# Reading a float32 accumulator back before the other one is complete: the tail of a routed-expert layer on one core

## The reference, cut to what matters

```python
hid = silu(x @ exp_w_gate[e]) * (x @ exp_w_up[e])          # 64 experts, 8 per token
routed = sum over e of (hid * gate[e]) @ exp_w_down[e]
shared = (silu(x @ shared_w_gate) * (x @ shared_w_up)) @ shared_w_down
x = x + g_f * (routed + shared)                            # g_f: one row per sequence
y = rmsnorm(x, final_norm_g)
```

## Time and profile before

| | us |
|---|---|
| three runs | 855.84, 860.97, 861.21 |
| median | 860.97 |
| profiled execution | 862.52 |
| its span in the trace | 860.6 |
| last weight load landed, about | 805.5 |
| last expert's down product (L1089) | 825.5 to 827.5 |
| first of the six reads issued | 834.62 |
| first final operation of VectorE (L1618) | 839.64 |
| last store issued (L387) | 857.32 |

### The profile page before, as it was taken

The page is one execution under the profiler, slowest core; times in us unless marked ns, Lnnn a source line. Parts: engine busy times, 40 slices in busy tenths (PEclk is TensorE's granted clock), DMA queues, the critical chain, the costliest instruction groups (busy, mean ns, idle before and its releaser), DMA issues.

```text
span 860.6 us, 14556 instructions
## 1 busy us (share of the span) xinstructions
PE 709.4 (82%) x4895; PEld 394.5 (46%) x4896; DVE 324.8 (38%) x617; ACT 227.9 (26%) x385; POOL 310.2 (36%) x331
## 2 busy tenths in 40 slices
PE   2599978999878979999789989988789868896830
PEld 1277553545535545554445545544355334443510
DVE  3105570646812463234142332333422423233217
ACT  4202621123022332233132222222322323232212
POOL 4001021021431663456352553545336443354130
PEclk9789989999879998999999999999999999999985
DMA  9979999308517999999999999999999999999333
GB/s 271 374 265 321 345 374 315 115 28 344 219 39 255 390 399 412 400 380 385 399 393 384 394 394 384 388 405 398 392 386 402 384 386 390 364 385 373 133 85 128
DMA packets 74658, 279.17 MB, mean 324 GB/s; under 512 B 19263, under 2 KB 22459, under 8 KB 48880
## 3 DMA queue, kind: packets, MB, share of 16 engines
q1 hardware_dynamic: 50082, 252.00, 74.5%
q0 software_dynamic: 23264, 26.07, 12.7%
q10 hardware_dynamic: 1262, 0.43, 0.2%
HBM read 272.28 MB, written 26.04 MB: 347 GB/s over the span
## 4 chain that ended last, share of the span: by engine, by line
PE 48%; DMA 43%; DVE 3%; issue 3%; SPq 1%; ACT 1%; POOL 0%; POOLq 0%; DVEq 0%
DMA gu<-in_exp_w_up 35%; PE bank L1053 18%; PE bank L1089 7%; PE bank L817 5%; PE bank L808 4%; DMA gu<-in_ada_w 4%; PE bank L935 3%; DMA gu<-in_w_in 2%; PE bank L1038 1%; PE bank L1135 1%; PE bank L820 1%; PE bank L783 1%; DMA sh<-acc_rows 1%; SPq L327 1%; PE bank L941 1%
## 5 line engine op out<-in xcount | busy, mean ns | idle before, releaser
L1053 PE MATMUL bank<-gu,et 128*64 128x256 f32 x2496 | 290.8, 389 | 59.6 <-DMA gu<-in_exp_w_up 53.8
L1053 PEld LDWEIGHTS bank<-gu,et 128*64 128x64 f32 x2496 | 183.4, 140 | 189.0 <-issue 113.5
L499 POOL DMA_INDIRECT acc_rows<-et,idx x64 | 104.6, 1634 | 283.5 <-DVE et L1544 197.6
L1089 PE MATMUL bank<-dn,et 128*64 128x512 f32 x624 | 150.3, 608 | 15.9 <-issue 13.7
L1537 DVE COPY et<-bank 128x256 f32<-128x256 f32 x64 | 27.2, 424 | 292.3 <-PE bank L1070 292.3
L706 ACT ACTIVATE et<-bank 64x512 f32<-64x512 f32 x64 | 37.9, 592 | 289.5 <-PE bank L1053 289.5
L1089 PEld LDWEIGHTS bank<-dn,et 128*64 128x64 f32 x624 | 41.6, 137 | 81.5 <-issue 80.9
L714 ACT ACTIVATE et<-bank,mb 128x512 f32<-128x512 f32 x64 | 44.0, 687 | 121.3 <-PE bank L1089 113.6
L1544 DVE TENSOR_SCALAR et<-bank,mb 128x512 f32<-128x512 f32 x64 | 48.1, 751 | 67.8 <-PE bank L1089 62.5
L1530 DVE TENSOR_TENSOR et<-et 64x512 f32<-64x512 f32 x64 | 67.9, 1061 | 0.4 <-ACT et L707 0.4
L509 POOL DMA_DIRECT2D small<-halfc x50 | 57.3, 1147 | 0.0
(11 more groups left out here) (279 smaller groups left out, 628.7 us busy)
## 6 DMA issues: line engine op xcount, KB each, us to landing
gu<-in_exp_w_gate SPq DMA_DIRECT2D x64, 1024.0 KB, 14.9
gu<-in_exp_w_up SPq DMA_DIRECT2D x64, 1024.0 KB, 29.6
dn<-in_exp_w_down SPq DMA_DIRECT2D x64, 1024.0 KB, 29.8
gu<-in_ada_w SPq DMA_DIRECT2D x12, 2048.0 KB, 17.4
gu<-in_w_in SPq DMA_DIRECT2D x3, 2048.0 KB, 19.3
gu<-in_w_out SPq DMA_DIRECT2D x2, 2048.0 KB, 28.9
acc_rows<-gn SPq DMA_DIRECT2D x2, 1280.0 KB, 17.1
gu<-in_w_in SPq DMA_DIRECT2D x2, 1024.0 KB, 19.6
```

What stands on the lines that cost most here:

```text
L499: pool.indirect_dma_start(acc_rows[u % 2], bass.IndirectOffsetOnAxis(ap=idx[:, u, 0:1], axis=0), yo[:, u % 2, 0, :], None, bounds_check=2 ...
L1053: mm = pe.matmul(bank[u % 2][64 * c:64 * c + 64, b * FE:(b + 1) * FE], xt[:, b, k % 4, k // 4, :], w[:, (c * KT + k) * FE:(c * KT + k + 1) ...
L1089: mm = pe.matmul(bank[5 + b][64 * c:64 * c + 64, :], hT[:, b, j, :], dn[:, dslot(u), j * D + c * HALF:j * D + (c + 1) * HALF], start=(j == ...
```

## The change

SP waits for the even accumulator's own semaphore, reads the even accumulator, all three tiles, into `sh`; then it waits for `routed` and reads the odd one into `xn`. The sum of the two doesn't depend on which is where. The wait within the branch for a second round of tokens (more than 128 for an expert) is only reached in such a round.

```diff
                     load_dn(r, NE // U - 1, U - 1)
+                    sync.wait_ge(scattered[0], 16 * NE * (r + 1))
                     if r + 1 < ROUNDS:
                         more_rounds(r + 1)
             more_rounds(1)
 
+            sync.wait_ge(s["pre_done"], 3)
+            sync.wait_ge(scattered[0], 16 * NE)
+            for t, (t0, n) in enumerate(TILES):
+                sync.dma_start(sh[0:n, t, :], acc_rows[0][2 * t0:2 * (t0 + n), :].rearrange("(p h) n -> p (h n)", h=2)).then_inc(acc_back[t], 16)
             sync.wait_ge(s["routed"], 1)
-            sync.wait_ge(s["pre_done"], 3)
             for t, (t0, n) in enumerate(TILES):
-                for b, dst in ((0, xn), (1, sh)):
-                    sync.dma_start(dst[0:n, t, :], acc_rows[b][2 * t0:2 * (t0 + n), :].rearrange("(p h) n -> p (h n)", h=2)).then_inc(acc_back[t], 16)
+                sync.dma_start(xn[0:n, t, :], acc_rows[1][2 * t0:2 * (t0 + n), :].rearrange("(p h) n -> p (h n)", h=2)).then_inc(acc_back[t], 16)
```

## The result

The changed kernel takes 860.76 us, the median of 20 runs (856.79 to 862.85), and the kernel before 857.0 us beside it (20 runs, 854.77 to 861.21). The ratio is 1.0039, 95% interval 1.0024 to 1.0054, so 2.1 to 4.6 us slower. The prediction said 0.9 us faster. The time itself is close to the 860.1 predicted, but that is luck: the first three runs of the kernel before (median 860.97), from whose median the 0.9 us were subtracted, lay above the median of its twenty.

The account below looks back on a forecast made before the run. Only the tail could change, bound by tile 1's start. Tile 0 0.15 us later and the idle 1.08 us gone put tile 1 0.9 us earlier: 860.1 us from the median of three runs, range 855.0 to 863.3.

Parts of the forecast that it names:

- What bounds the tail: End of kernel: tile 1's start, the later of VectorE free from tile 0 and tile 1's reads, plus 16.1 us.
- wait in front of tile 1: VectorE's idle time between tiles 0 and 1, awaiting a read into `sh`; forecast to go, worth 1.08 us.
- The start of the even reads: SP's first even read, released by expert 62's second scatter: issued about 832.1 in place of 834.62, 2.5 us earlier.
- Tile 0: First final operations on VectorE, needing the first and fourth reads: start 839.8, ends 838.2 and 841.2, before 839.64.
- half rate: Third tile's 64-partition even read, ahead of tile 0's odd read: 0.26 MB at 200 instead of 350 GB/s, 0.6 us more.
- Rival A: Early start arrives in full at 426 GB/s: tile 0 at 838.2, 2.5 us gained, 858.5; chance 0.15.
- Rival B: Three even reads ahead move tile 0 to about 840.7, paying back the 1.08 us: 861.0; chance 0.25 with D.
- lags: Reads landing behind their nominal ends at 350 GB/s: 1.2, 1.0, 1.5 and 3.0 us for the four full reads.
- Rival C: Even reads delay expert 63's small copy, hence `routed`; tile 0 starts 3.4 us later, +2.3 us, 863.3; chance 0.15.

Follow-up runs that it names:

- l_pool2: Kernel before with even reads of tiles 0 and 1 early, tile 0's even half worked off first, third tile's three final operations on GpSimd: ratio 1.0035.
- e_wait: Kernel before with a wait for the even semaphore added ahead of the wait for `routed`, no read moved: ratio 0.9981.
- b_dead: Kernel before with one more wait, in the never entered branch for a second round; no executed instruction changes: ratio 1.0002.
- m_after: The changed kernel once more, beside other runs of the kernel before: ratio 1.0025.
- d_order: Kernel before with only the new order, all six reads after `routed`, three even then three odd, nothing early: ratio 1.0029.
- i_actqueue: Changed kernel without the wait in the branch, odd reads on ScalarE's queue instead of SP's: ratio 1.0023 to the kernel before.
- c_nodead: Changed kernel without the wait in the never entered branch for a second round: ratio 1.0027 to the kernel before.
- h_t01early: Kernel before with even reads of tiles 0 and 1 early, then odd 0, odd 1, even 2, odd 2 after `routed`: ratio 1.0.
- j_order2: Kernel before with all six reads after `routed`, ordered even 0, even 1, odd 0, odd 1, even 2, odd 2: ratio 1.001.
- n_last: Kernel before with all six reads after `routed`, tile 0's odd read last of all: ratio 1.0088.

## Why the prediction was wrong, point by point

**What bounds the tail** held: tile 1 starts when VectorE has done tile 0 or its own reads are in, and from there on the length is fixed. After, 841.48 to the end of the span is 16.1 us, as before. The wait in front of tile 1 went, as forecast, in every kernel that read the even half first, but for `l_pool2` (1.06 us). What it is worth was taken from one execution, though: the old order shows 1.11 us in the kernel before, 1.53 in `e_wait` and none in `b_dead`.

**The start of the even reads** was forecast 2.5 us ahead of the first read of before. In one execution it was (offset 2.48 in `m_after`), in the profiled one it was 1.26 us (3.81 against 5.07), since expert 62's scatter took 5.6 us to land and not 4.4. That is most of this execution's error in tile 0 (1.3 of 1.5 us): one row doesn't give the range of a wait.

**Tile 0 was the step that failed:** "I take 839.8, nearest to the case with the half rate, with 838.2 and 841.2 as ends." That is offset 10.25, at most 11.65. Measured: 11.74, 12.87 and 14.32. Take it as a start and a length. From the first issue to tile 0 I had 7.7 us (832.1 to 839.8). `d_order`, where nothing is early, took 7.98 (830.88 to 838.86), so for a stream that begins when the scatters are over the sum was right, with the third tile's read in the way (1.35 us by my terms, 0.75 for its bytes and 0.6 for its half rate; 1.6 measured). What failed is the credit for the head start: I let this length begin 2.5 us earlier and kept it. Set against the 2.96 us that the order costs, tile 0 came 1.65, 2.18 (`i_actqueue`), 2.78 and 4.23 us later than before, so the head start gave back 1.3, 0.8 and 0.2 us, and in `m_after` it cost 1.3. These are differences of single executions, so the sizes are rough. In the profiled execution the length was 7.93 us, but the start came 1.3 us later than forecast. Where the start did come early, the length grew: 9.82 us with a start at offset 3.05 (`c_nodead`, 831.04 to 840.86) and 11.84 with 2.48 (`m_after`, 827.56 to 839.40). Between a head start that doesn't come and one that is lost on the way, nothing was left to pay for the third and fourth place of the odd read.

Against a gain of at most 1.08 us from the wait in front of tile 1, a tile 0 that comes 1.65 to 4.2 us later gives a loss of 0.6 to 3.2 us. Set against the means of the old order (tile 1 at 14.66, after at 16.64), it is 2.0 us.

**Rival A** is out: its rate was reached (426 GB/s), its tile 0 at offset 8.65 in no kernel. **Rival B** named the right thing, the three even reads ahead, and stopped at a price of zero; its own lags of up to 3.0 us, which it cited, would have carried it past 840.7. I had put the upper end of tile 0 at 841.2, already on the slow side, and took the middle.

**Rival C** forecast the right sign and nearly the right size (+2.3 us), but by another mechanism, and that one is refuted at its price. It wanted the small copy to land 2.5 us late. In the five kernels whose trace shows `routed` beside early reads it came at offset 4.17 to 5.50, with the copy landing in at most 4.5 us (`h_t01early`); in the six without early reads at 4.40 to 5.07. In the changed kernel and `c_nodead`, where SP was still issuing, it came no later than 6.1 and 4.8. What the Trainium skill says in "DMA: Bandwidth & Descriptors", section "Queues, rings and completion order", of engines taking turns between queues isn't seen at work in `i_actqueue`: by turns I expected tile 0 at 9.5 to 11 there, and it came at 12.27. That the copy's completion write waits for even reads in flight no run here shows.

**The half rate.** By the Trainium skill, page "SBUF — State Buffer", section "Door 1: The DMA port swizzle", 64 partitions reach half of the ports. The 213 GB/s at the end of `j_order2` agree with it; the 147 to 188 in `n_last` are lower still, and full reads moved in that stretch too. For this read the rule and its price were about right (0.6 us, 0.8 measured in one pair of traces); what I didn't draw from them was that this one read, set ahead of the odd one, costs more (1.6 us) than the wait in front of tile 1 that goes (1.08 us).

**What stays open.** The tail accounts for about 2.0 us of a loss measured at 2.1 to 4.6 us in the first comparison and 0.3 to 4.1 in the later two. Whether a part of the first lies elsewhere can't be told from these. Nor is it shown why the first odd read took 5.6 us in one execution and 10.1 in another of the same kernel. A slow first read explains a part of it at most: in `c_nodead` the first one took 3.5 us, and the second 7.0 where `d_order` has 4.5. That reads issued before offset 3 meet busy engines is seen; that this is the reason for the longer streams is only argued. And why none of the kernels with tails of 28.5 to 29.8 us is faster than the kernel before stays open.

## What to carry to other kernels

A transfer that must wait for the last result gets no earlier because others went ahead of it; here it got later. Where a consumer needs one transfer of each group, order them so that each of its inputs is complete as soon as can be, whether or not a group can start early. Narrow transfers (64 partitions) belong behind the wide ones that somebody waits for, since a read of theirs delayed what was behind it by twice what its bytes are worth (1.6 against 0.75 us, in one pair of traces). And with tails that vary by 1.6 to 2.6 us from execution to execution, one profile can show a mechanism but not its size: the first one after the change showed 0.47 us of a loss of 3.3.

## What the runs showed of the hardware that I had not expected

Float32 operations of GpSimd and VectorE on SBUF at the same time slowed each other: from 1.23 to 3.36 us for 128x1024 on VectorE, from 2.33 to 3.2 for 64x1024 on GpSimd, one waiting for the other to end (`l_pool2`). The issue of a DMA on SP's queue can take 2.37 us with reads in flight, against 0.35 on an idle queue. The first read took 4.3 to 6.6 us when it went out within 3 us of the last scatter's issue, and 3.3 to 3.7 later. And in the new order it took 7.98 us from the first issue to tile 0 with nothing early, and 7.93, 9.82, 9.37 and 11.84 us with a start 0.6, 1.35, 1.5 and 1.9 us earlier (`d_order`, the changed kernel, `c_nodead`, `i_actqueue`, `m_after`).
